# A two-direction RWKV recurrence: the triangular solve done beside its squarings, fewer and wider matmuls, steps without a loop

## The chip, the core and the metric

The program runs on one core of one Trainium2 chip. The metric is the time of one execution in device microseconds (us). Everything is float32. A float32 matmul stands in the program as one instruction and in the trace as two records (two MATMUL and two LDWEIGHTS); a transpose has one record of each.

## What is computed

The reference is two blocks in a row: a two-layer hybrid attention block, then a two-layer block with neighbourhood attention, an RWKV-7 mixer and two mixtures of experts. The change is inside the RWKV mixer of the second layer. It runs this step over 256 context tokens and then 512 latent tokens, in both directions, for 16 heads of 64, and uses outputs y of the latent tokens alone:

```python
def _rwkv_step(S, inp):
    r, w, kk, kka, kt, v = inp
    sk = jnp.einsum('bhij,bhj->bhi', S, kk)
    S = S * w[:, :, None, :] - sk[..., None] * kka[:, :, None, :] + v[..., None] * kt[:, :, None, :]
    return S, jnp.einsum('bhij,bhj->bhi', S, r)
...
        S_f, y_f = _rwkv_scan(S0[0], (r, w[0], kk, kk * a[0], kt[0], v), False)
        S_b, y_b = _rwkv_scan(S0[1], (r, w[1], kk, kk * a[1], kt[1], v), True)
        return (S_f, S_b), (y_f + y_b, r, kt, v, g)
...
    ctx_state, ctx_feats = stream(hc, None)
    _, lat_feats = stream(hl, ctx_state)
```

Here w is a decay per channel, kk the normalised key, a a learned rate, and `kka` is `kk * a`.

## The kernel before

`rwkv_layer` calls `rwkv_scan`, in which four engines work on chunks of 64 tokens (CH = 64): 4 of context, then 8 of latents, for each of two directions z, so 24 pairs of chunk and direction. The 16 heads are 8 pairs (PAIRS); two heads lie on partitions 0 to 63 and 64 to 127, and a product of all heads is 16 matmuls of 64x64 blocks (`heads`, line 2301, and `pair`, line 2290; line 2297 is the matmul itself). The work of one pair of chunk and direction has three parts.

- **front**: decays and rates of the chunk. `decay_rank` (L2339) and `rate_rank` (L2347) are low-rank products, `cumulate` (L2358) sums log-decays along the chunk, DVE adds biases (L2581, L2586), ACT takes sigmoids and exponentials with a table load ahead of each kind (L2500, L2511), and DVE and POOL scale keys and queries (L2594 to L2615, L2239 to L2248, L2260).
- **chain**: within a chunk the recurrence is a triangular system (I - N)X = X0, with N of 64x64 for each head. `gram` makes N and its transpose M from the keys, DVE masks them (L2647). Five `level` steps square them: each is 32 matmuls, 16 for the powers of N and 16 for those of M, and ACT (L2522) and DVE (L2651) copy the result from PSUM. POOL adds the identity to each power (`factor`, L2234), which gives the factors I + M^(2^n). `rows` turns keys by 32 matmuls with an identity, `raised_n` and `raised_r` are further grams.
- **tail**: `start` makes X0 from the carried state and the values; six `apply` steps multiply the factors into X one after another, each of 16 matmuls, an ACT copy (L2517) and the next; then `results` gives y and `state` the new state, which DVE adds (L2644) and POOL decays (L2253).

The order is written out by hand. A **slot** (the function `both`) holds the chain of one direction, the tail of the other and the front of the other's next chunk; each engine has its own list of the same steps. There are two slots per chunk, one for each direction. A hardware loop (`eng.Fori`, in `in_turn`, around L2185) runs two slots a turn, once over the context and once over the latents, with slots before and after each loop that fill and empty the pipeline. In a loop a semaphore wait is against a register value, and on PE each wait also adds to a semaphore `begun`; POOL copies the chunk's columns to fixed places first (L2220, L2222, L2227), since the loop's addresses change:

```python
            both(None, 0, 0, None, 0)
            both(0, 0, 1, None, 0)
            with eng.Fori(0, steps - 1) as it:
                both(1, it, 0, it, it + 1)
                both(0, it + 1, 1, it, it + 1)
            both(1, steps - 1, 0, steps - 1, None)
            both(None, 0, 1, steps - 1, None)
```

After the scan `rwkv_readout` normalises y and adds `bonus` times the values, and then output projection and experts follow. Stages are divided by a barrier of all engines, so the scan overlaps with no other stage.

## Time and profile before

| | |
|---|---|
| median of 3 runs | 4123.04 us (4122.61 to 4123.76) |
| the profiled execution, its own time | 4099.76 us |
| span of its trace | 4098.0 us |
| of it, the scan stage (2562.4 to 3376.2 us) | 813.8 us |
| mean granted TensorE clock | 0.91 |
| PE busy, DVE, ACT, POOL | 82%, 36%, 20%, 11% |

A stretch is named by its start and end in us from the span's start. A record's time is from its start to its modelled end, and matmuls overlap, so the time a group takes is read from its start to the start of what follows. The number in brackets at a row's end is the idle time of the engine before it and what ended it; "issue" is idle time for which the profile shows no awaited event. The granted clock is 1.00 at 2.4 GHz and 0.50 at 1.2 GHz.

### The profile page before, as it was taken

How to read it: one execution, taken by the hardware profiler on the slowest of the kernel's cores; microseconds unless marked ns; L12 is line 12 of the kernel's file. 1: busy time of each engine (PE TensorE's matmuls, PEld its weight loads, DVE VectorE, ACT ScalarE, POOL GpSimd, SP SyncE). 2: the span in 40 equal slices, each digit the busy share in tenths (PEclk: the TensorE clock that was granted, in tenths of full speed). 3: DMA queues.
4: the chain of work that ended last, by engine and by line, in shares of the span. 5: the costliest groups of instructions: out<-in, count | busy, mean ns of one | idle time of the engine just before them, and what ended most of it. 6: DMA issues, size and time to landing. Idle time of an engine off the chain costs nothing. (4 is left out here: it accounts for less than half of the span.)

```text
span 4098.0 us, 85586 instructions
## 1 busy us (share of the span) xinstructions
PE 3343.7 (82%) x37286; PEld 1973.3 (48%) x37286; DVE 1463.6 (36%) x3061; ACT 811.7 (20%) x1666; POOL 462.1 (11%) x448
## 2 busy tenths in 40 slices
PE   6998999896999986999995898776777765678877
PEld 5846476463445643343342444666666662322222
DVE  3656256552025623212213412443444434311111
ACT  2015111241015610000001001443333320100000
POOL 0000000000001100000000000443433320000000
PEclk9998899988999987999997998897989877799999
DMA  5652247302111124999996110000000002299998
GB/s 163 164 186 74 50 118 190 117 22 83 57 48 33 60 82 176 365 346 336 363 345 228 49 48 21 4 4 3 4 4 4 4 13 100 100 399 404 404 402 347
DMA packets 148963, 606.63 MB, mean 148 GB/s; under 512 B 19200, under 2 KB 21824, under 8 KB 131584
## 3 DMA queue, kind: packets, MB, share of 16 engines
q1 hardware_dynamic: 142272, 579.57, 39.0%
q0 software_dynamic: 6336, 21.63, 2.3%
q8 instruction: 308, 5.05, 0.5%
q14 instruction: 47, 0.39, 0.0%
HBM read 576.39 MB, written 31.07 MB: 148 GB/s over the span
## 5 line engine op out<-in xcount | busy, mean ns | idle before, releaser
L1704 PE MATMUL psum<-ring,big 128*64 128x512 f32 (+1 forms) x6144 | 904.8, 500 | 110.2 <-DMA ring<-moe_w 93.6
L1704 PEld LDWEIGHTS psum<-ring,big 128*64 128x64 f32 (+1 forms) x6144 | 301.4, 125 | 674.4 <-issue 472.6
L2297 PE MATMUL psum<-ring 64*64 64x64 f32 x11520 | 250.4, 232 | 100.8 <-issue 75.5
L371 PE MATMUL psum<-h_uT,ring 128*128 128x264 f32 x1280 | 290.5, 387 | 0.0
L2297 PEld LDWEIGHTS psum<-ring 64*64 64x64 f32 x11520 | 218.6, 143 | 129.2 <-issue 117.9
L371 PEld LDWEIGHTS psum<-h_uT,ring 128*128 128x128 f32 x1280 | 242.0, 190 | 46.5 <-issue 5.8
L500 DVE SCALAR_TENSOR_TENSOR h_O<-h_O,cond_silu 128x512 f32<-128x512 f32 x336 | 227.1, 743 | 102.2 <-DMA h_O<-ada_w 102.2
L1215 PE MATMUL psum<-ring,big 128*128 128x512 f32 x576 | 251.1, 596 | 2.0 <-PEq L55 2.0
L1985 PE MATMUL psum<-big,ring 128*128 128x512 f32 (+1 forms) x464 | 171.4, 532 | 31.7 <-DVE big L1956 24.0
L1850 DVE TENSOR_TENSOR big<-big,psum 128x512 f32<-128x512 f32 (+1 forms) x48 | 27.3, 596 | 463.7 <-PE psum L1704 463.7
L2234 POOL TENSOR_TENSOR ring<-ring,eye_sb 128x512 f32<-128x512 f32 x120 | 154.0, 1283 | 222.8 <-PE psum L2297 221.5
L1215 PEld LDWEIGHTS psum<-ring,big 128*128 128x128 f32 x576 | 109.0, 191 | 134.8 <-issue 134.8
L391 PE MATMUL psum<-ring,h_uT 128*128 128x512 f32 x384 | 168.3, 595 | 0.0
L2517 ACT ACTIVATE ring<-psum 128x512 f32<-128x512 f32 x168 | 100.4, 598 | 336.3 <-PE psum L2297 333.1
L1858 DVE SCALAR_TENSOR_TENSOR big<-psum,big,gates 64x512 f32<-64x512 f32 (+1 forms) x128 | 78.8, 615 | 242.8 <-PE psum L1704 241.4
L1001 PE MATMUL psum<-ring,big 128*128 128x512 f32 x320 | 141.3, 605 | 11.0 <-DMA ring<-rw_w_o 9.4
L1985 PEld LDWEIGHTS psum<-big,ring 128*128 128x128 f32 x464 | 90.0, 195 | 112.9 <-issue 108.8
L1784 ACT ACTIVATE big<-psum 128x512 f32<-128x512 f32 (+1 forms) x48 | 23.5, 524 | 566.8 <-PE psum L1704 566.7
L2651 DVE COPY ring<-psum 128x512 f32<-128x512 f32 x96 | 66.4, 691 | 173.7 <-PE psum L2297 173.7
L391 PEld LDWEIGHTS psum<-ring,h_uT 128*128 128x128 f32 x384 | 72.0, 190 | 90.2 <-issue 90.1
L119 PE MATMUL psum<-ident_sb,big 128*128 128x128 f32 x176 | 29.0, 343 | 97.0 <-DVE big L197 97.0
L1001 PEld LDWEIGHTS psum<-ring,big 128*128 128x128 f32 x320 | 61.9, 194 | 89.1 <-issue 79.6
(344 smaller groups left out, 4544.7 us busy)
## 6 DMA issues: line engine op xcount, KB each, us to landing
ring<-moe_w SPq DMA_DIRECT2D x192, 2048.0 KB, 10.8
h_O<-ada_w SPq DMA_DIRECT2D x192, 256.0 KB, 3.0
ring<-w_in SPq DMA_DIRECT2D x16, 2048.0 KB, 14.8
ring<-na_w_qkv SPq DMA_DIRECT2D x6, 2048.0 KB, 8.0
ring<-w_out SPq DMA_DIRECT2D x4, 2048.0 KB, 8.8
bias_rows<-na_table SPq DMA_DIRECT2D x16, 480.0 KB, 15.7
ring<-bias_rows SPq DMA_DIRECT2D x16, 360.0 KB, 2.9
rows<-big SPq DMA_DIRECT2D x10, 512.0 KB, 5.1
```

The lines of the kernel that those rows point to most:

```text
L371: last = nc.tensor.matmul(bank(k, pair_bank(q) + h, NH), w[:, a, f * P:(f + 1) * P], uT[:, a, halves[h]], start=a == 0, stop=a == KD - 1)
L391: last = nc.tensor.matmul(bank(k, b), uT[:, a, t * P:(t + 1) * P], w[:, a, :], **st)
L500: nc.vector.scalar_tensor_tensor(into, ada(u), by, into, ALU.mult, ALU.add).then_inc(s.acc, 1)
L1001: last = nc.tensor.matmul(bank(k, j % BANKS)[0:rows, :], srcT[:, a, t * P:t * P + rows], w[:, a, :], start=a == 0, stop=a == KD - 1)
L1215: last = nc.tensor.matmul(bank(k, j % FIRST_BANKS), hT[:, a, t * P:(t + 1) * P], w[:, a, :], start=a == 0, stop=a == KD - 1)
L1704: last = nc.tensor.matmul(bank(k, b, r.width)[q * r.n:(q + 1) * r.n, :], rowsT[:, half * HALF_K + n, r.first:r.first + r.n], w[:, n, q * r ...
L1858: last = nc.vector.scalar_tensor_tensor(y[r.first:r.first + r.n, x % 2, cols], bank(k, r.downs, r.width)[mine, :], gate[mine, x, 2 * r.at ...
L1985: last = nc.tensor.matmul(bank(k, j % BANKS, n), w[:, a, at:at + P], xs[m][:, a, first:first + n], **st)
L2234: ev["pool"][z].done(nc.gpsimd.tensor_tensor(pairs(factors[n], z), pairs(factors[n], z), eye3, ALU.add), f"factor{n}")
L2297: last = nc.tensor.matmul(bank(k, b, CH, at + p % QUAD * CH)[to:to + CH, :], pairs(lhs, z)[lo:lo + CH, p, :], rhs(lo, p), start=start and ...
L2517: ev["act"][z].done(nc.scalar.activation(flat2(T_n, z), side(W(z), 0), ACT.Copy), f"x{n}")
L2651: ev["dve"][z].done(nc.vector.tensor_copy(both_of(n, z, 1), bank(k, U(z) + 1).rearrange("p (e x) -> p e x", e=2)), f"level{n}")
```

## The change

- The solve is X <- X + M X beside the squaring of M and N: `level` n multiplies M by N and X, which lie side by side (one matmul of 128 columns per head block), and 16 matmuls of 64 columns give the next M. There are six levels; level 5 has X and M alone, level 6 X alone. The six `apply` steps and POOL's `factor` are gone. DVE adds the product to X in three operations (`step`), ACT copies M and N.
- `gram_m` and `raised` take alpha and rho side by side in 128 columns for latents; `gram_n` is a product of its own. `rows` is 8 transposes of 128x128 and six ACT copies in place of 32 matmuls and two copies. Bonus sums are 4 matmuls of 2 columns in place of 16 of one column.
- The loop, the register waits, `begun` and POOL's column copies are gone: all steps stand in the program one by one, with constant waits. The pipeline isn't emptied between context and latents. A slot now holds the solve of one direction (i), and of the other results and state (j), grams and start of the next chunk (n) and the front's first part of the one after (m).
- y and bonus are written by the first direction that comes to a chunk and added to by the second, so their fills are gone. `rwkv_readout` has four small ACT copies that put the bonus sums in order, for which POOL waits. Two more constant tables are loaded.

```diff
-            with eng.Fori(0, steps - 1) as it:
-                both(1, it, 0, it, it + 1)
-                both(0, it + 1, 1, it, it + 1)
...
+        def in_turn(slot):
+
+
+            here = lambda t: t if 0 <= t < ROUNDS else None
+            slot(1, None, None, 0, None, None, 0)
+            slot(0, None, 0, 1, None, None, 0)
+            slot(1, None, 0, 0, None, 0, 1)
+            for t in range(ROUNDS):
+                slot(0, t, here(t + 1), 1, here(t - 1), t, here(t + 1))
+                slot(1, t, here(t + 1), 0, t, here(t + 1), here(t + 2))
+            slot(0, None, None, 1, ROUNDS - 1, None, None)
...
-                def factor(z, it, n):
-
-                    after("pe", z, it, f"level{n + 1}")
-                    ev["pool"][z].done(nc.gpsimd.tensor_tensor(pairs(factors[n], z), pairs(factors[n], z), eye3, ALU.add), f"factor{n}")
-                    after("pool", z, it, f"factor{n}")
...
-                        last = nc.tensor.matmul(bank(k, b, CH, at + p % QUAD * CH)[to:to + CH, :], pairs(lhs, z)[lo:lo + CH, p, :],
-                                                rhs(lo, p), start=start and n == 0, stop=stop and n == len(terms) - 1)
+                        last = nc.tensor.matmul(bank(k, b, width, at + p % QUAD * width)[to:to + CH, :], lhs(lo, p), rhs(lo, p),
+                                                start=start and n == 0, stop=stop and n == len(terms) - 1)
...
-            pe.wait_ge(s.cleared, 3)
-            for lat, steps, first, chunk, ev, fr in phase_list():
-                def wait(sem, value):
-                    pe.wait_ge(sem, value)
-
-                    pe.sem_inc(s.begun, 1)
...
+            def gram_m(z, t):
+                made("dve", z, t, "rho" if lat(t) else "beta")
+                if lat(t):
+                    last = heads(W(z), 0, (beta(z), both(AR, z)), width=2 * CH)
+                else:
+                    last = heads(W(z), 0, (beta(z), alpha(z)))
+                ev["pe"][z].done(last, t, "gram_m")
...
+                for n, src in enumerate((T_beta, T_kappa)):
                     for i in range(QUAD):
...
+                        last = nc.tensor.transpose(bank(k, U(z) + n, P, i * P), own(src, z)[:, i * P:(i + 1) * P], k.ident[:, :])
+                ev["pe"][z].done(last, t, "rows")
...
+            def gram_n(z, t):
+                after("act", z, t, "rows")
+                ev["pe"][z].done(heads(U(z), 0, (alpha(z), beta(z))), t, "gram_n")
+
+            def level(z, t, n):
+
+
+                if n == 1:
+                    after("dve", z, t, "mask_n")
+                    after("dve", z, t, "x0")
+                else:
+                    after("dve", z, t, f"x{n - 1}")
+                    after("act", z, t, f"N{n - 1}" if n < LEVELS else f"M{n - 1}")
+                m = plain(T_m, z)
+                if n < LEVELS - 1:
+                    heads(U(z), 0, (m, with_x(z, n % 2 == 0)), width=2 * CH)
+                    last = heads(W(z), 0, (n_of(z), m))
+                elif n < LEVELS:
+                    heads(U(z), 0, (m, x_alone(z, n % 2 == 0)))
+                    last = heads(W(z), 0, (n_of(z), m))
+                else:
+                    last = heads(U(z), 0, (m, x_alone(z, n % 2 == 0)))
+                ev["pe"][z].done(last, t, f"level{n}")
...
-                def apply(z, it, n):
-                    after("act", z, it, f"x{n}")
-                    if n == 0:
-                        after("dve", z, it, "x0")
-                    if n < LAST:
-                        after("pool", z, it, f"factor{n}")
-                    else:
-                        after("dve", z, it, f"factor{n}")
-                    ev["pe"][z].done(heads(W(z), 0, z, (factors[n], of(T_n, z))), f"apply{n}")
...
-                def level(z, it, n):
-                    if n == 1:
-                        after("dve", z, it, "mask_m")
-                        made("pool", z, it, "end")
-                    else:
-                        after("act", z, it, f"level{n - 1}")
-                        after("dve", z, it, f"level{n - 1}")
-                    if n < LAST:
-                        heads(U(z), 0, z, (factors[n - 1], of(T_n, z)))
-                        last = heads(U(z), SIDE, z, (T_n, of(factors[n - 1], z)))
-                    else:
-                        last = heads(U(z), 0, z, (T_n, of(factors[n - 1], z)))
-                    ev["pe"][z].done(last, f"level{n}")
...
-                    if lat:
-                        made("dve", z, it, "rho")
-                    heads(W(z), 0, z, (T_beta, eye))
-                    ev["pe"][z].done(heads(W(z), SIDE, z, (T_kappa, eye)), "rows")
...
+            def slot(z, i, f, y, j, n, m):
+                if j is not None:
+                    results(y, j)
+                if n is not None and lat(n):
+                    bonus_sum(y, n)
+                if j is not None:
+                    state(y, j)
+                if i is not None:
+                    level(z, i, 1)
+                if m is not None:
+                    low_rank(y, m, j, n)
+                if i is not None:
+                    level(z, i, 2)
+                if n is not None:
+                    gram_m(y, n)
+                if i is not None:
+                    level(z, i, 3)
+                if m is not None:
+                    cumulate(y, m)
+                if i is not None:
+                    level(z, i, 4)
+                if n is not None:
+                    raised(y, n)
+                if i is not None:
+                    level(z, i, 5)
+                if n is not None:
+                    rows(y, n, j, m)
+                    start(y, n, j)
+                if i is not None:
+                    level(z, i, 6)
+                if n is not None:
+                    gram_n(y, n)
+
+            in_turn(slot)
...
+            def level(z, t, n):
+
+                after("pe", z, t, f"level{n}")
+                ev["act"][z].done(copy(groups(T_m, z), side(W(z), 0)), t, f"M{n}")
+                if n < LEVELS - 1:
+                    after("dve", z, t, f"xa{n}")
+                    copy(N(z)[:, 0, :, :], woven(U(z), 0)[:, 0, :, :])
+                    after("dve", z, t, f"x{n}")
+                    ev["act"][z].done(copy(N(z)[:, 1, :, :], woven(U(z), 0)[:, 1, :, :]), t, f"N{n}")
...
+            def rows(z, t):
+                after("pe", z, t, "rows")
+                for n, (to, sign) in enumerate(((T_brow, -1.0), (T_krow, 1.0))):
+                    got = bank(k, U(z) + n).rearrange("p (a h x) -> p h a x", h=2, x=CH)
+                    for rows, src, h in ((slice(0, P), slice(0, P), 0), (slice(CH, P), slice(0, CH), 1), (slice(0, CH), slice(CH, P), 1)):
+                        last = nc.scalar.activation(pairs(to, z)[rows, h * QUAD:(h + 1) * QUAD, :], got[src, h, :, :], ACT.Identity, scale=sign)
+                ev["act"][z].done(last, t, "rows")
+
+            def x_first(z, t):
+                after("pe", z, t, "start")
+                ev["act"][z].done(copy(X(z), side(W(z), 0)), t, "x0")
...
+            def step(z, t, n):
+                after("pe", z, t, f"level{n}")
+                got = woven(U(z), 1) if n < LEVELS - 1 else side(U(z), 0)
+                x = X(z)[:, 0, :, :]
+                ev["dve"][z].done(tt(x, x, got[:, 0, :, :], ALU.add), t, f"xa{n}")
+                if n == 1:
+                    after("dve", z, t, "x0")
+                else:
+                    after("dve", z, t, f"x{n - 1}")
+                old, new = x_of_side(z, n % 2 == 0), x_of_side(z, n % 2 == 1)
+                for h in range(2):
+                    here, there = slice(h * CH, (h + 1) * CH), slice((1 - h) * CH, (2 - h) * CH)
+                    last = tt(new[there], old[here], got[there, 1, :, :], ALU.add)
+                ev["dve"][z].done(last, t, f"x{n}")
+
```

PE, the middle of a latent slot in the loop of before: from level 4 to the end of the level 5 that closes the squarings; ring and gates hold the factors and keys, `head_ones_sb` is the bonus sum.

```order
L2297 MATMUL psum<-ring 64x64 x32
L2319 REGISTER_ALU x2
L2297 MATMUL psum<-ring 64x64 x16
L2319 REGISTER_ALU
L2297 MATMUL psum<-gates 64x64 x16
L2441 MATMUL psum<-head_ones_sb,ring 64x1 x16
L2319 REGISTER_ALU x2
L2297 MATMUL psum<-ring 64x64 x16
L2319 REGISTER_ALU
L2297 MATMUL psum<-ring 64x64 x16
```

PE, a latent slot in the program after: from level 1 to the end of `raised` and level 5's beginning; ring holds N and X, gates holds M, L2301 is the second low-rank product and L2312 is `cumulate`.

```order
L2256 MATMUL psum<-ring,gates 64x128 x16
L2256 MATMUL psum<-gates,ring 64x64 x16
L2297 MATMUL psum<-ring,X 64x512 x2
L2301 MATMUL psum<-X,ring 128x64 x8
L2256 MATMUL psum<-ring,gates 64x128 x16
L2256 MATMUL psum<-gates,ring 64x64 x16
L2256 MATMUL psum<-big,ring 64x128 x16
L2256 MATMUL psum<-ring,gates 64x128 x16
L2256 MATMUL psum<-gates,ring 64x64 x16
L2312 MATMUL psum<-running_sb,X 128x128 x8
L2256 MATMUL psum<-ring,gates 64x128 x16
L2256 MATMUL psum<-gates,ring 64x64 x16
```

Each level is now a row of 128 columns and a row of 64, with one step of the other direction between two levels, and no register instruction stands between.

DVE, the same loop of before: from `iclr` over a level's copy and `m` and `kt` to the next level's copy.

```order
L2586 TENSOR_TENSOR X<-psum,a_cols_sb 128x512
L2571 REGISTER_ALU
L2651 COPY ring<-psum 128x2x256
L2571 REGISTER_ALU
L2574 ISA
L2594 SCALAR_TENSOR_TENSOR ring<-X,ka_cols_sb 128x512
L2574 ISA
L2596 ISA
L2596 SCALAR_TENSOR_TENSOR ring<-ring,big 128x512
L2571 REGISTER_ALU
L2651 COPY ring<-psum 128x2x256
```

DVE, a latent slot after: step 1, then `dec`, `iclr`, `m`, `kt` and step 2.

```order
L2592 TENSOR_TENSOR ring<-ring,psum 128x4x64
L2600 TENSOR_TENSOR ring<-ring,psum 64x256 x2
L2522 TENSOR_TENSOR X<-psum,ring 128x512
L2527 TENSOR_TENSOR ring<-psum,a_cols_sb 128x512
L2535 SCALAR_TENSOR_TENSOR ring<-ring,ka_cols_sb 128x512
L2537 SCALAR_TENSOR_TENSOR ring<-ring,big 128x512
L2592 TENSOR_TENSOR ring<-ring,psum 128x4x64
L2600 TENSOR_TENSOR ring<-ring,psum 64x4x64 x2
L2586 TENSOR_TENSOR gates<-psum,before_less_sb 128x512
```

A level's single copy of 512 columns has become an addition of 256 columns on 128 partitions and two on 64 partitions, and four operations of the fronts stand between step 1 and step 2.

## Rows read from the trace of the kernel before

**Rows 1.** Stretches: length, busy (records) of PE, PEld, DVE, ACT, POOL; clock, DMA.

```profile
2562.40:2621.70 59.30, 42.50 (x1353) 36.41 (x1354) 28.62 (x39) 25.51 (x39) 26.25 (x26) 0.82 0.01 3
2621.70:2758.00 136.30, 100.81 (x4037) 89.23 (x4032) 63.09 (x86) 63.53 (x100) 53.96 (x56) 0.95 0.02 4
2758.00:2867.50 109.50, 76.21 (x2685) 67.42 (x2680) 41.54 (x60) 38.63 (x60) 41.25 (x39) 0.78 0.01 3
2867.50:3353.60 486.10, 352.50 (x13939) 319.81 (x13941) 206.56 (x317) 173.12 (x273) 182.68 (x178) 0.88 0.02 4
3353.60:3376.20 22.60, 12.64 (x383) 11.30 (x377) 2.98 (x6) 4.18 (x7) 2.06 (x2) 0.62 0.01 2
```

**Rows 2.** DMA queues, 2867.5 to 3353.6: packets, MB, share.

```profile
q8 instruction: 124, 2.03, 1.6%
```

**Rows 3.** PE in order of time, latent slot: start, length, group, count.

```profile
3057.76 1.20 PE L2297 MATMUL psum<-ring 64*64 64x64 f32 x46 [1.25 <-issue]
3059.05 1.16 PE L2358 MATMUL psum<-running_sb,ring 64*128 64x128 f32 x16
3060.14 1.15 PE L2297 MATMUL psum<-ring 64*64 64x64 f32 x60
3062.05 1.16 PE L2297 MATMUL psum<-ring 64*64 64x64 f32 x36 [0.76 <-issue]
3063.00 0.68 PE L2297 MATMUL psum<-big,gates 64*64 64x64 f32 x32
3063.47 0.67 PE L2297 MATMUL psum<-gates,big 64*64 64x64 f32 x32
3064.20 0.57 PE L2297 MATMUL psum<-ring 64*64 64x64 f32 x23
3066.21 1.53 PE L2297 MATMUL psum<-ring 64*64 64x64 f32 x73 [1.43 <-issue]
```

**Rows 4.** Who PE waited for, 2867.5 to 3353.6: us, times, longest.

```profile
PE psum L2297 <- issue: 68.2, 59, 2.1
```

**Rows 5.** PE at full clock in the first slots.

```profile
2581.61 2.00 PE L2347 MATMUL psum<-rw_tac,ring 64*128 64x64 f32 x16
2583.54 1.16 PE L2297 MATMUL psum<-ring 64*64 64x64 f32 x64
2584.52 0.65 PE L2297 MATMUL psum<-eye_sb,big 64*64 64x64 f32 x32
```

**Rows 6.** Transposes, `results`, `state`, `start`, first low-rank product.

```profile
33.77 6.66 PE L119 MATMUL psum<-ident_sb,h_O 128*128 128x128 f32 x39 [33.77 <-DVE h_O L197]
...
2567.41 1.97 PE L2339 MATMUL psum<-ring,rw_twc 64*64 64x512 f32 x4 [6.77 <-POOL rw_twc L2220]
...
3072.53 0.39 PE L2297 MATMUL psum<-X,gates 64*64 64x64 f32 x6 [0.80 <-ACT ring L2517]
...
3075.99 0.35 PE L2297 MATMUL psum<-X,big 64*64 64x64 f32 x7
...
3077.43 0.27 PE L2297 MATMUL psum<-X 64*64 64x64 f32 x2 [0.97 <-issue]
...
3078.47 0.34 PE L2297 MATMUL psum<-X 64*64 64x64 f32 x5
```

**Rows 7.** An `apply` alone, last slot: copy, then the next product.

```profile
3362.22 0.60 ACT L2517 ACTIVATE ring<-psum 128x512 f32<-128x512 f32 x1 [1.49 <-PE psum L2297]
...
3363.11 1.13 PE L2297 MATMUL psum<-ring 64*64 64x64 f32 x32 [0.95 <-ACT ring L2517]
```

**Rows 8.** Groups, by form: busy us, mean ns, idle before.

```profile
L2651 DVE COPY ring<-psum 128x512 f32<-128x512 f32 x96 | 66.4, 691 | 173.7 <-PE psum L2297 173.7
...
L1445 ACT ACTIVATE ring<-psum 128x256 f32<-128x256 f32 x32 | 10.3, 367 | 1.2 <-PE psum L1360 1.2
...
L2009 DVE COPY big<-psum 64x256 f32<-64x256 f32 x24 | 10.1, 422 | 73.3 <-PE psum L1982 73.1
L2640 DVE TENSOR_TENSOR ring<-ring,psum 128x256 f32<-128x256 f32 x24 | 10.1, 419 | 59.5 <-ACT ring L2517 59.5
```

786 lines of the change are left out of this document (347 added, 439 removed).

## Prediction

> **What bounds the kernel now.** I read the stretches first, then the queue of the DMA, then PE in order of time. The scan is a stage of its own, 2562.4 to 3376.2, 813.8 us [rows 1]; nothing else is touched but for trifles, so what it gains the kernel gains. Its slots can be counted by PE's records: a context slot has 402 matmuls, 804 records, so 4037 records in 136.3 us are 5 slots of 27.3 us; a latent slot has 498 matmuls, 996 records, so 13939 records in 486.1 us are 14 slots of 34.7 us [rows 1]. Between them, 109.5 us hold three slots, in which one loop ends and the other fills.
>
> PE has work for little more than 60% of a latent slot. Sixty-four records of 64x64 blocks, four blocks at a time, take 0.98 us from their start to that of the next group [rows 5], so 16 matmuls take 0.48 and 32 take 0.98. With the low-rank products at 1.97 and 1.93 [rows 5, 6], `results` and `state` at 3.46 with a short gap within, taken as 3.2, `start` at 2.82 less 0.97 idle = 1.85 [rows 6], and `cumulate` at 1.09 (3059.05 to 3060.14) [rows 3], the list of before sums to 3.2 + `gram` 0.98 + levels 4 x 0.98 + 0.48 + `rows` 0.98 + `raised_n` 0.98 + `raised_r` 0.9 + `apply` 6 x 0.48 + 3.9 + 1.09 + 1.85 = 21.2 us at full clock. The slot takes 34.7.
>
> The rest is in the gaps put down to "issue". They come in the middle of groups in which nothing is awaited, and evenly: 46 + 16 + 60 = 122 matmul records lie between the gap that ends at 3057.76 and that at 3062.05, and 36 + 32 + 32 + 23 = 123 between that and 3066.21 [rows 3]. With their weight loads that is some 245 instructions, and the instruction queue moved 124 packets in 486.1 us, 2.03 MB, 16.4 KB each [rows 2]. At 64 bytes an instruction (an estimate from 16.4 KB and the 256 that the gaps suggest) each is a page of 256. So PE gets a page each 3.92 us, uses it up in some 2.3 us where all is dense, and stands for the rest: 68.2 us in 59 gaps, 1.16 us each [rows 4]. A latent slot takes 124 / 14 = 8.9 pages, and 8.9 x 3.92 is 34.7: the whole slot. The supply of instructions bounds the loop, and the waits of the solve lie hidden in it.
>
> **Part 1: fewer instructions.** A latent slot after has 366 matmul instructions, 8 of them transposes: 358 x 4 + 8 x 2 = 1448 records, and the register instructions are gone (8.9 x 256 = 2270 less 1992 leaves 280 of them before). With some 30 waits that is 5.8 pages, 22.7 us by 3.92. A context slot has 314: 1270, 5.0 pages, 19.5 us. Pages alone would no longer bound either.
>
> **Part 2: PE's work.** Sixteen matmuls of 128 columns cost at least 0.48 (as many instructions as the narrow ones) and about 0.98 at most (the columns of 32 narrow ones) [rows 5]. I take 0.92, near the upper end, since the columns double and only weight loads are saved. Eight transposes of 128x128: 6.66 / 39 = 0.17 each [rows 6], 1.4 in all, 0.4 more than the 32 matmuls of before. Latent slot: 3.2 (`results`, `state`) + 0.3 (bonus, between 0.1 and 0.6) + levels 1 to 4 at 0.92 + 0.48 each, 5.6, + 0.98 + 0.48 + 3.9 + `gram_m` and `raised` 1.84 + 1.09 + 1.4 + 1.85 + `gram_n` 0.48 = 21.1. So PE's work stays what it was; context 21.1 - 2.1 (`results`) - 0.3 - 0.88 = 17.8.
>
> **Part 3: the waits that take the place of the gaps.** Level n + 1 needs X and N of level n: 0.06 us from PE's end to the copy, and 0.29 from the copy's end (3362.82) to the next product (3363.11) [rows 7]. Between them now stand three DVE additions of 256 columns, one on 128 and two on 64 partitions, at 0.42 each, and the last ACT copy of 256 columns, 0.37 [rows 8]: 0.06 + 1.26 + 0.37 + 0.29 = 1.98, and 0.16 more, by which a group of 16 matmuls ends after the next could start (0.65 against 0.49) [rows 5]: 2.14. What stands between on PE hides part of it. Level 1 to 2: the low-rank products, 3.9, hide all. Level 2 to 3: `gram_m` 0.92 hides all but 1.22, and DVE comes late by about 0.6, since `iclr`, `m` and `kt` stand ahead of step 2. Level 3 to 4: `cumulate`, 1.04 left. Level 4 to 5: `raised`, 1.22 left. Level 5 to 6: transposes and `start` hide all. At the end, ACT has six copies for `rows` and one for X0, DVE adds X0 and only then takes step 6, and `results` waits for that, some 1.5. Together 5.6: 26.7 us. In a context slot `gram_m` and `raised` hide 0.44 less each: 17.8 + 6.5 = 24.3.
>
> **Part 4: what is left of the page limit.** From `start` over level 6, `gram_n`, `results`, bonus and `state` to the end of level 1 there are 180 matmuls, 720 instructions, 2.8 pages, 11.0 us, against 1.85 + 0.96 + 1.5 + 3.5 + 1.4 = 9.2 us of work and wait: 1.8 more. In a context slot 128 matmuls, 2.0 pages, 7.8 against 6.8: 1.0. Elsewhere a page holds wide matmuls and waits and lasts about 4 us anyway. The granted clock was 0.88 in the latent stretch, 0.95 in the context [rows 1]; PE will stand less, and I add 0.3 and 0.2. So a latent slot is **28.8 us** and a context slot **25.5 us**.
>
> **Part 5: ends of the pipeline.** Before, the first state came 59.3 us after the stage's start [rows 1]. After, the fills of y and bonus go, but three filling slots stand first; with the first solve I put the first state there as well, so 35 us ahead of the first of 24 solving slots. At the end only results, state and y are left, 6 us. The turn between the loops is two ordinary slots and more in before, none of it lost in after. POOL loses `factor` and the column copies, off the path. The ACT copies in the readout are under 0.4 each and POOL, which waits, has nothing behind it that is late; two table loads and they cost 1 us at most.
>
> Sum: 35 + 8 x 25.5 + 16 x 28.8 + 6 = 706 us against 813.8, 108 less. The profiled execution took 4099.76 and would take 3992. The median of the runs is 4123.04, 0.6% above it, and the same difference from it gives **4015 us**.
>
> **Where the Trainium skill disagrees.** The Trainium skill ("Runtime: NRT & Kernel Launch", Instruction fetch mechanics) says that crossing into the next 16 KiB block is mostly hidden by the fetch ahead, and that a taken branch is what stalls it. The gaps in the loop show otherwise: a turn is two slots, 17.7 pages, with one jump, and a gap stands at nearly every page [rows 2, 3]. By that rule the gaps would leave with the loop.
>
> **Rivals.**
> - *The gaps belong to the loop.* Its jumps and register instructions make them, and straight code has none. Then part 4 falls away: slots of 27.0 and 24.5, 35 + 196 + 432 + 6 = 669, **3978 us**. For it: all gaps that I read lie in a loop. Against it: their even distance. Then each of 5.8 pages costs its 1.2 us beside the waits: 26.7 + 0.3 + 7.0 = 34.0, and 24.3 + 0.2 + 6.0 = 30.5: 35 + 244 + 544 + 6 = 829, **4138 us**. It decides from about 5.5 us of gaps in a mean slot: (813.8 - 41) / 24 = 32.2, against 26.1 without gaps. For it: in before, work and gaps do add up to most of the slot. Against it: a wait within a page gives the fetch time.
> - *DVE's narrow additions cost as much as wide ones*, 0.69 for 0.42 [rows 8], by their strides and by waits in DVE's order. A step is 0.8 longer, at four places: 32.0 and 28.7, 35 + 230 + 512 + 6 = 783, **4092 us**. Against it: both rows of 256 columns.
> - *All falls well.* Wide products at 0.48, no page limit, full clock: 24.9 and 22.5, 35 + 180 + 398 + 6 = 619, **3928 us**.
>
> **Chances.** Forecast 0.55 (3975 to 4060 of its own), gaps of the loop 0.12, DVE's price 0.12, gaps added 0.11, all well 0.10. The range reaches from part of the last case over the first three to 4100 and leaves out 4138: 3950 to 4100. About 0.2%, 8 us, is what a measurement tells from no change. Faster by more 0.86, within it 0.03 (between DVE's price and the added gaps), slower 0.11.
>
> **What the profile after would show.** Part 1: 5.8 and 5.0 packets of instructions a slot. Part 2: PE's records of 128 columns, 32 in about 0.92 us, and 8 transposes in 1.4. Part 3: PE waiting for DVE's `step` or ACT's N copy at levels 3, 4 and 5 and ahead of `results`, 1.1 to 1.9 us each. Part 4: gaps of "issue" between `start` and level 1, and few between levels. I am wrong if gaps of 1.2 us stand at every page still, if DVE is busy for most of a slot, or if the clock falls below 0.8.

## The result, and the profile after

The kernel after takes **3940.9 us** (median of four runs, 3931.4 to 3953.5) against 4123.4 (four runs, 4122.6 to 4124.0): a ratio of 0.9559, with a 95% interval of 0.9526 to 0.9593. The forecast was 4015 with a range from 3950; the time lies 9 us below the range. The direction and the engine that bounds were right, the gain is 182 us where 108 were forecast.

Its profiled execution took 3932.92 us, span 3931.1. The scan goes from 2561.8 to 3215.7: 653.9 us against 813.7, so 160 of the 167 us between the two profiled executions are there. The windows of both scans and of the stretches after, with the columns of [rows 1]; the first is of before, the others of after (the whole scan; five slots, nearly all of them context; thirteen latent slots, the first twelve of them full):

```profile
2562.40:3376.10 813.70, 584.66 (x22368) 524.16 (x22368) 342.78 (x504) 304.96 (x479) 306.19 (x299) 0.87 0.02 4
```

```profile
2561.80:3215.70 653.90, 503.71 (x16544) 450.01 (x16544) 411.16 (x816) 330.80 (x647) 116.57 (x105) 0.94 0.01 3
...
2628.30:2748.10 119.80, 88.94 (x3100) 79.77 (x3100) 75.68 (x152) 69.12 (x136) 14.80 (x16) 0.96 0.01 3
...
2798.50:3146.90 348.40, 277.38 (x9371) 250.29 (x9372) 232.85 (x466) 176.86 (x348) 74.97 (x66) 0.96 0.01 4
```

A slot is best counted from one decay of the state to the next, POOL's operation on `d_end` (once a slot). POOL in order of time, after: the first slot, the beginning and the end of twelve full latent slots, and the last two.

```profile
2628.30 1.04 POOL L2211 TENSOR_TENSOR X<-X,rw_d_end 128x512 f32<-128x512 f32 x1
...
2798.49 1.04 POOL L2211 TENSOR_TENSOR X<-X,rw_d_end 128x512 f32<-128x512 f32 x1
...
3122.81 1.04 POOL L2211 TENSOR_TENSOR X<-X,rw_d_end 128x512 f32<-128x512 f32 x1
...
3191.05 1.04 POOL L2211 TENSOR_TENSOR X<-X,rw_d_end 128x512 f32<-128x512 f32 x1 [24.98 <-DVE X L2583]
3214.63 1.04 POOL L2211 TENSOR_TENSOR X<-X,rw_d_end 128x512 f32<-128x512 f32 x1 [22.54 <-DVE X L2583]
```

(3122.81 - 2798.49) / 12 = **27.0 us** a full latent slot, where 28.8 was forecast. Those in which the granted clock stays at 1.00 take 26.0 to 26.2, those at 0.94 take 27.5. The seven slots ahead take 24.3 on average (25.5 forecast), the shortest of them 23.0, and the last four 23.0 on average (17.9 to 26.3), since less and less of a front is in them (28.8 forecast, as if they were full).

The queue of instructions, 2748.1 to 3144.4 (15 slots, 12 of them full), against 124 packets in 486.1 us [rows 2]; and whom PE waits for there, against 68.2 us of "issue" [rows 4]:

```profile
q8 instruction: 84, 1.38, 1.4%
```

```profile
PE psum L2256 <- ACT ring L2443: 52.9, 46, 2.0
PE psum L2256 <- DVE ring L2600: 20.8, 13, 1.6
PE psum L2256 <- ACT X L2480: 6.1, 15, 0.4
```

The gaps that nothing ended are gone. What stands in their place are the waits of the solve: for ACT's copy of N (L2443), for DVE's step 6 (L2600) ahead of `results`, and a new short one for ACT's copies of rows (L2480). PE in order of time in one latent slot shows them one by one, beside the prices of the new shapes [rows 5]:

```profile
2957.32 1.10 PE L2256 MATMUL psum<-ring,gates 64*64 64x128 f32 x32 [1.46 <-ACT ring L2443]
2958.24 0.64 PE L2256 MATMUL psum<-gates,ring 64*64 64x64 f32 x32
2958.81 1.16 PE L2312 MATMUL psum<-running_sb,X 64*128 64x128 f32 x16
2960.82 1.10 PE L2256 MATMUL psum<-ring,gates 64*64 64x128 f32 x32 [0.84 <-ACT ring L2443]
...
2964.31 0.69 PE L2256 MATMUL psum<-ring,gates 64*64 64x64 f32 x32 [1.05 <-ACT ring L2443]
...
2965.40 1.09 PE L2348 MATMUL psum<-ident_sb,ring 128*128 128x128 f32 x8
2966.42 0.36 PE L2256 MATMUL psum<-X,big 64*64 64x64 f32 x8
...
2968.92 0.69 PE L2256 MATMUL psum<-ring,big 64*64 64x64 f32 x32 [0.41 <-ACT X L2480]
2971.21 0.39 PE L2256 MATMUL psum<-X,big 64*64 64x64 f32 x6 [1.60 <-DVE ring L2600]
...
2973.22 1.05 PE L2320 MATMUL psum<-head_ones_sb,X 128*128 128x2 f32 x8
2974.20 0.34 PE L2256 MATMUL psum<-ring,X 64*64 64x64 f32 x8
...
2976.53 0.61 PE L2297 MATMUL psum<-ring,X 64*64 64x512 f32 x2
...
2977.49 2.00 PE L2301 MATMUL psum<-X,ring 64*128 64x64 f32 x16
2979.41 1.10 PE L2256 MATMUL psum<-ring,gates 64*64 64x128 f32 x32
```

The waits are 1.46 + 0.84 + 1.05 + 0.41 + 1.60 = 5.4 us of 26.0. The bonus sums (L2320) take 0.98 us (2973.22 to 2974.20) for matmuls of two columns. PE's weight loads show why: the other side of each is 128x128, and loading it fills that time.

```profile
2973.22 0.97 PEld L2320 LDWEIGHTS psum<-head_ones_sb,X 128*128 128x128 f32 x8
```

### The profile page after: what moved, and what is told of

Read it like the earlier page. It is cut to its first block and busy times, and to the rows that moved or that the text cites. A ratio compares the mean times of both kernels' runs of the same rounds, so it can differ in the third digit from the quotient of the medians.

```text
span 3931.1 us, 72090 instructions
## 1 busy us (share of the span) xinstructions
PE 3256.2 (83%) x31462; PEld 1895.5 (48%) x31462; DVE 1528.8 (39%) x3373; ACT 838.0 (21%) x1838; POOL 276.4 (7%) x254
## 5 line engine op out<-in xcount | busy, mean ns | idle before, releaser
L1704 PE MATMUL psum<-ring,big 128*64 128x512 f32 (+1 forms) x6144 | 902.6, 500 | 115.2 <-DMA ring<-moe_w 99.0
L2256 PE MATMUL psum<-ring,gates 64*64 64x128 f32 (+1 forms) x5120 | 177.2, 265 | 96.5 <-ACT ring L2443 94.1
L2256 PEld LDWEIGHTS psum<-ring,gates 64*64 64x64 f32 x5120 | 140.0, 141 | 111.0 <-DVE ring L2600 108.4
L1215 PEld LDWEIGHTS psum<-ring,big 128*128 128x128 f32 x576 | 109.0, 191 | 134.8 <-issue 134.8
L1784 ACT ACTIVATE big<-psum 128x512 f32<-128x512 f32 (+1 forms) x48 | 23.5, 524 | 565.5 <-PE psum L1704 565.5
L2600 DVE TENSOR_TENSOR ring<-ring,psum 64x256 f32<-64x256 f32 x288 | 120.9, 420 | 6.4
L2443 ACT ACTIVATE gates<-psum 128x512 f32<-128x512 f32 x120 | 71.6, 596 | 236.0 <-PE psum L2256 236.0
L1790 ACT ACTIVATE big<-psum 128x512 f32<-128x512 f32 (+1 forms) x48 | 25.2, 526 | 399.8 <-PE psum L1727 399.8
L2256 PE MATMUL psum<-big,ring 64*64 64x64 f32 (+1 forms) x2816 | 110.3, 249 | 0.0
```

The source lines that it names most:

```text
L1215: last = nc.tensor.matmul(bank(k, j % FIRST_BANKS), hT[:, a, t * P:(t + 1) * P], w[:, a, :], start=a == 0, stop=a == KD - 1)
L1704: last = nc.tensor.matmul(bank(k, b, r.width)[q * r.n:(q + 1) * r.n, :], rowsT[:, half * HALF_K + n, r.first:r.first + r.n], w[:, n, q * r ...
L2256: last = nc.tensor.matmul(bank(k, b, width, at + p % QUAD * width)[to:to + CH, :], lhs(lo, p), rhs(lo, p), start=start and n == 0, stop=st ...
L2443: copy = lambda out, got: nc.scalar.activation(out, got, ACT.Copy)
L2600: last = tt(new[there], old[here], got[there, 1, :, :], ALU.add)
```

## Experiments

Two theories stand against each other for the kernel before: **P**, the forecast's, that PE is held by the supply of instruction pages wherever its code is dense, and **L**, that the gaps belong to the loop. For the kernel after, **S** says that the chain of the solve sets the slot. Times are medians, ratios to the kernel before, run on the same chip beside them. The groups of runs stood on different chips: the kernel before took 4123.4 us beside after, 4132.9 beside E1 to E4, 4124.1 beside E5 to E8 and 4132.4 beside E9 to E11. So across groups the ratios count and not the medians; 0.001 of a ratio is 4.1 us.

| | us | ratio (95%) | scan, us | clock in it |
|---|---|---|---|---|
| before, first profile / second (E9) | 4123.4 | 1 | 813.7 / 844.6 | 0.87 / 0.83 |
| after | 3940.9 | 0.9559 (0.9526 to 0.9593) | 653.9 | 0.94 |
| E1 before, written out | 4080.6 | 0.9865 (0.9844 to 0.9886) | 796.5 | 0.87 |
| E2 before, four slots a turn | 4074.2 | 0.9856 (0.9832 to 0.9881) | 792.4 | 0.88 |
| E3 after, narrow | 3982.0 | 0.9628 (0.9603 to 0.9652) | 694.3 | 0.93 |
| E4 after, M first | 3864.9 | 0.9344 (0.9324 to 0.9363) | 585.5 | 0.95 |
| E5 as E4, step 6 first | 3849.8 | 0.9338 (0.9313 to 0.9362) | 554.0 | 0.97 |
| E6 after, DVE early | 3923.4 | 0.952 (0.9491 to 0.9549) | 636.7 | 0.92 |
| E7 after, less DVE | 3882.4 | 0.942 (0.9392 to 0.9449) | 595.0 | 0.97 |
| E8 after, dense | 4082.2 (one run) | | 794.4 | 0.95 |
| E10 after, `m` and `kt` first | 3941.2 | 0.9542 (0.9519 to 0.9566) | 660.6 | 0.92 |
| E11 as E5 and E10 | 3844.2 | 0.9313 (0.9294 to 0.9332) | 558.4 | 0.96 |

### E1: the loop alone

```diff
-            with eng.Fori(0, steps - 1) as it:
+            for it in range(steps - 1):
                 both(1, it, 0, it, it + 1)
                 both(0, it + 1, 1, it, it + 1)
```

> The kernel before, with the scan's hardware loops written out: the same matmuls in the same order, constants in the place of register values in the waits; the increments of `begun` and the copies of columns stay. A latent slot is then 1992 matmul instructions and some 70 waits and increments, 2060, or 8.05 pages of 256 (8.9 before); a context slot 1670, 6.5 pages. Theory P (the prediction's: a page of instructions each 3.92 us, wherever the code stands): slots of 31.5 and 25.6 us against 34.7 and 27.3, the scan about 750 us against 813.8, the kernel 0.984 of before; gaps of issue still stand at nearly every page, some 1.1 us each. Theory L (the gaps belong to the loop): the gaps that no event ends leave PE almost wholly, 68.2 us of them in 14 slots, 4.9 us a slot; what they hid of the waits comes back in part. Slots of 29 to 30 us, the scan 700 to 730, the kernel 0.975 to 0.982; issue gaps under 10 us in the 14 slots, and pages that follow each other sooner than 3.9 us where the code is dense.

The kernel gains 1.35%, 52 us by the medians of one chip. The gaps stay. Whom PE waits for in 14 latent slots (2869.1 to 3336.1) of E1:

```profile
PE psum L2297 <- issue: 82.2, 71, 2.1
PE psum L2339 <- POOL rw_twc L2220: 20.9, 13, 2.1
PE psum L2297 <- ACT ring L2517: 11.1, 14, 0.8
PE psum L2441 <- issue: 8.7, 5, 1.9
PE psum L2358 <- issue: 2.8, 2, 1.4
```

Together 93.7 us of issue in 14 slots, in code without one jump, against 68.2 + 17.8 = 86.0 in before (the row of the sums of bonus, below, belongs to [rows 4]). Theory L falls: the gaps don't belong to the loop. 110 packets in these slots are 7.9 pages a slot, as counted (8.05). But P's times missed too: the scan is 796.5 us where P said 750, a latent slot 33.4 where it said 31.5. The pages came 4.25 us apart on average (467.0 / 110) and not 3.92, and beside the gaps stand 33 us of waits for POOL, ACT and DVE. So the gaps belong to the supply of pages, but the supply doesn't set the whole slot.

P's account of the gain doesn't hold either. It came from 0.85 page a slot of register instructions. Of before, the same stretch as [rows 4], the other rows:

```profile
PE psum L2441 <- issue: 17.8, 13, 1.6
PE psum L2297 <- POOL rw_tac L2222: 12.2, 3, 4.3
...
PE psum L2297 <- POOL rw_twc L2220: 10.7, 3, 3.7
```

and PE around one turn of the loop:

```profile
2966.66 0.33 PE L2297 MATMUL psum<-X,ring 64*64 64x64 f32 x6
2971.29 0.51 PE L2297 MATMUL psum<-X,big 64*64 64x64 f32 x8 [4.29 <-POOL rw_tac L2222]
```

Each turn of the loop stands for some 4 us, six times in these slots, 22.9 us. The profile names POOL's copy, but the group that starts is `start`, which doesn't wait for that copy. Over the whole scan the profile puts eight such stands, 30.3 us, down to POOL's copies, one for each of the eight jumps back. In E1 these stands are gone, and part of them comes back elsewhere in the 14 slots: PE waits 20.9 us for POOL's copy ahead of the low-rank product (9.1 before), and issue gaps are 7.7 us more. By the Trainium skill ("Runtime: NRT & Kernel Launch", Instruction fetch mechanics) a taken branch whose target lies outside the two pages at hand forces a fetch of it before execution goes on; a stand of 4 us at each turn agrees with it, and is about what one page takes in E8 (3.74 us). The same section's rule that crossing a 16 KiB block is mostly hidden does not agree with E1's 93.7 us in straight code.

### E2: half the jumps

```diff
-            with eng.Fori(0, steps - 1) as it:
-                both(1, it, 0, it, it + 1)
-                both(0, it + 1, 1, it, it + 1)
+            both(1, 0, 0, 0, 1)
+            both(0, 1, 1, 0, 1)
+            with eng.Fori(0, (steps - 2) // 2) as turn:
+                for u in (1, 2):
+                    it = turn * 2 + u
+                    both(1, it, 0, it, it + 1)
+                    both(0, it + 1, 1, it, it + 1)
```

> The kernel before, with four slots in a turn of the loop and not two, so half the jumps back (the first two slots of each loop are written out ahead of it). P: nothing changes but for trifles, a page still takes 3.92 us: 0.998 to 1.002 of before. If it is the jump that stops the supply: half of the gaps go, 2.4 us a slot, 40 to 50 us of the kernel, 0.988 to 0.990. If anything in a loop is supplied late, however long the turn: no change in the loop's slots, but the slots written out run without gaps, some 3 us less each, four of them: 0.996 to 0.998.

All three expectations missed: 59 us less by the medians, as much as without a loop. The two loops jump back twice in place of eight times (2 + 6), so six jumps less were worth as much as eight within the measurement, which doesn't tell them apart. The gaps of issue in the latent slots (76.2 + 1.8 us in 14 slots) are near those of before, so a jump has its own price, beside the pages and not instead of them: two stands of this kind are left in the scan for the two jumps, 8.1 us, where before had eight and 30.3. The instruction queue moved 182 packets in the scan, E1's 179 and before 194: 12 less for six jumps, so a jump also costs some two pages fetched for nothing. The stands account for 22 us of the 59. The scans of the profiled pair differ by 21 us against the first profile of before and by 52 against the second (E9), and the second difference is mostly PE's busy time at a higher granted clock (574.6 us at 0.88 against 612.4 at 0.83); why the clock is higher no run shows.

### E3: more instructions for the same columns

```diff
-                        last = nc.tensor.matmul(bank(k, b, width, at + p % QUAD * width)[to:to + CH, :], lhs(lo, p), rhs(lo, p),
-                                                start=start and n == 0, stop=stop and n == len(terms) - 1)
+                        for e in range(width // CH):
...
+                            last = nc.tensor.matmul(bank(k, b, CH, at + p % QUAD * width + e * CH)[to:to + CH, :], lhs(lo, p), r,
+                                                    start=start and n == 0, stop=stop and n == len(terms) - 1)
```

> The kernel after, with each matmul of 128 columns split into two of 64 on the same weights: 96 more matmuls in a latent slot, 384 instructions, 1.5 pages more (7.1), 64 more in a context slot, 1.0 page (5.8 to 6). P: a page each 3.92 us gives 27.8 us for a latent slot against 26.4, and the dense stretch from start to the end of level 1 gets 0.25 page longer; with gaps of issue back: 20 to 35 us more than after. L, with the solve's waits as the bound: only PE's work grows, 32 blocks of 64 columns in 0.98 us against 0.92, six times, 0.4 us or less a slot, some of it behind waits: 0 to 10 us more than after, no issue gaps.

41 us slower than after by the medians, 28 by the ratios (0.9628 against 0.9559: 0.0069 x 4123; the kernel before was 10 us slower beside E3), the scan 40 us longer. Gaps of issue are back. Some twelve latent slots of E3 (2798 to 3146):

```profile
PE psum L2260 <- ACT ring L2447: 21.7, 25, 1.5
PE psum L2260 <- issue: 20.8, 27, 2.0
PE psum L2260 <- DVE ring L2604: 18.8, 12, 1.6
PE psum L2316 <- issue: 3.3, 3, 1.3
PE psum L2305 <- issue: 1.1, 1, 1.1
```

That is the upper end of P's 20 to 35 and beyond by the medians, within it by the ratios. 25.2 us of gaps in 348, and 87 packets, a page each 4.0 us. Part of the gaps lies where the waits for ACT were (21.7 us here; 45.0 in the same stretch of after). P holds, and says what the wide products are worth: not PE's work (0.92 against 0.98 for a group) but a quarter of the instructions.

### E4: the chain shortened, M first

```diff
+                if n < LEVELS:
+                    ev["pe"][z].done(heads(W(z), 0, (n_of(z), m)), t, f"m{n}")
+                after("dve", z, t, f"x{n - 1}")
                 if n < LEVELS - 1:
-                    heads(U(z), 0, (m, with_x(z, n % 2 == 0)), width=2 * CH)
-                    last = heads(W(z), 0, (n_of(z), m))
+                    last = heads(U(z), 0, (m, with_x(z, n % 2 == 0)), width=2 * CH)
...
-                after("pe", z, t, f"level{n}")
-                ev["act"][z].done(copy(groups(T_m, z), side(W(z), 0)), t, f"M{n}")
+                after("pe", z, t, f"m{n}")
+                ev["act"][z].done(copy(groups((T_m, T_m2)[n % 2], z), side(W(z), 0)), t, f"M{n}")
```

> The kernel after, with each level's product for M ahead of that for N and X, a second buffer for M (so that ACT copies M beside the second product), and ACT's copy of N in the order that keeps clear of DVE (the far half first). The values are the same. Theory S (the chain of the solve, from a product's end over ACT and DVE to the next, sets the slot): the next product can begin when N is there, 0.37 + 0.37 + 0.06 + 0.29 = 1.1 us after the level's end, and X, ready 1.6 after it, is awaited behind 0.48 of work; before it was 2.1. The waits ahead of levels 3, 4 and 5 (1.46, 0.84, 1.05) fall by up to 1.0, 0.84 and 1.0: a latent slot of 23.6 to 24.4 us against 26.4, a context slot 21.5 to 22.5 against 24.0, 45 to 65 us less than after. P: 5.6 pages by 3.92 are 22.0, but the dense stretches grow, and gaps of issue come back: a latent slot not under 25, 20 to 30 us less than after.

The second buffer for M lies over the gate that the projection after the scan multiplies with, so that what follows the scan works on other values, at the same cost. 76 us less than after by the medians, 89 by the ratios (0.9344 against 0.9559), 68 in the scan: the way S says, and more than its 45 to 65. The edit holds three things (M first, its second buffer, the order of ACT's copies), which no run takes apart. Full latent slots take 23.7 to 24.3 us for the most part, as S says, and context slots 20.7, less than its 21.5 to 22.5. PE in order of time around `raised` and the end of a slot:

```profile
2975.85 0.69 PE L2256 MATMUL psum<-gates,ring 64*64 64x64 f32 x32 [0.44 <-ACT ring L2440]
...
2982.97 0.59 PE L2256 MATMUL psum<-X,big 64*64 64x64 f32 x6 [1.60 <-DVE ring L2599]
...
2995.54 0.69 PE L2256 MATMUL psum<-gates,ring 64*64 64x64 f32 x32 [0.48 <-ACT ring L2440]
```

Level 3 waits 0.48, level 4 nothing and level 5 0.44, in place of 1.46, 0.84 and 1.05: 2.4 us less a slot. Hardly a gap of issue comes back (0.3 us in 375), so after had room down to this. `results` still waits 1.60.

### E5: step 6 ahead of X0

```diff
+                if i is not None:
+                    step(z, i, 6)
                 if n is not None:
                     after("act", y, n, "x0")
                     x = joint(NX, y, 1)[:, QUAD:, :]
                     ev["dve"][y].done(tt(x, x, bank(k, W(y), SIDE, SIDE).rearrange("p (a x) -> p a x", x=CH), ALU.add), n, "x0")
-                if i is not None:
-                    step(z, i, 6)
```

> The same as the kernel with the product for M first, but the second buffer for M lies in columns of Y and V that are free at that time (in the former run it lay over a gate that a later stage needs), and DVE takes step 6 of the one direction ahead of the addition to X0 of the other. Theory S: `results`, which waited 1.60 us for step 6 in each slot, finds it ready 0.42 us of addition and some 0.7 us of waiting for ACT's copy sooner: 1.0 us less in each of 23 slots, 20 to 26 us less than the former run's 3865. Theory P, with the shortest distance of two pages seen so far, 3.35 us, as the true price: 5.6 pages are 18.8 us, still under the slot, but between `start` and the end of level 1 2.8 pages are 9.4 us, and with a wait of 0.5 in the place of 1.6 the work there is 9.0: gaps of 0.4 us come back in some slots, and 10 to 16 us are left of the gain.

3849.8 us. The wait ahead of `results` falls from 1.60 to 0.50, as S says:

```profile
2910.20 0.69 PE L2262 MATMUL psum<-ring,big 64*64 64x64 f32 x32 [0.23 <-ACT X L2483]
2911.39 0.39 PE L2262 MATMUL psum<-X,big 64*64 64x64 f32 x6 [0.50 <-DVE ring L2605]
```

The scan is 31.5 us shorter than E4's, of which 1.1 us in 23 slots are 25. The kernel is 15 us faster by medians from two chips, but the ratios, 0.9338 against 0.9344, differ by 2 us and their intervals overlap, and the profiled execution (3834.0) was the fastest of the five. So the profile shows the wait shrink, and the timed runs don't show that the kernel gains by it. The expected 20 to 26 us aren't borne out. A full latent slot takes 22.6 to 23.9 us.

### E6: DVE doesn't wait for the product of M

```diff
-                    heads(U(z), 0, (m, with_x(z, n % 2 == 0)), width=2 * CH)
+                    ev["pe"][z].done(heads(U(z), 0, (m, with_x(z, n % 2 == 0)), width=2 * CH), t, f"u{n}")
...
-                after("pe", z, t, f"level{n}")
+                after("pe", z, t, f"u{n}" if n < LEVELS else f"level{n}")
```

> The kernel after, with one event more a level: DVE takes up its step when the product for N and X is done and doesn't wait for the product for M behind it. ACT still waits for both. S: DVE is 0.48 us sooner where it isn't busy, and the chain is then ACT's: copy of M 0.60, two of N 0.37 each, 1.34 after the level's end, against 1.63; 0.28 less at levels 4 and 5, nothing at level 3, where DVE comes late from `m` and `kt`, 0.3 less ahead of `results` no (level 6 has one product): 0.5 to 0.6 us a slot, 10 to 15 us less than after. If PE isn't bound by this chain: no change.

17.5 us less than after by the medians, 16 by the ratios, somewhat above the 10 to 15 of S; the intervals of the two ratios overlap a little, so the gain is likely and not certain. Level 4 waits 0.37 and level 5 0.58, so 0.47 less each where 0.28 was reckoned, and level 3 as before:

```profile
2898.36 1.10 PE L2256 MATMUL psum<-ring,gates 64*64 64x128 f32 x32 [1.45 <-ACT ring L2443]
2901.39 1.10 PE L2256 MATMUL psum<-ring,gates 64*64 64x128 f32 x32 [0.37 <-ACT ring L2443]
2904.41 0.69 PE L2256 MATMUL psum<-ring,gates 64*64 64x64 f32 x32 [0.58 <-ACT ring L2443]
2911.31 0.39 PE L2256 MATMUL psum<-X,big 64*64 64x64 f32 x6 [1.59 <-DVE ring L2600]
```

I had added ACT's durations, but its operations overlap: in the profile of after a copy of N starts 0.49 us after a copy of M that lasts 0.60.

### E7: one addition less a step

```diff
-                for h in range(2):
+                for h in range(1):
                     here, there = slice(h * CH, (h + 1) * CH), slice((1 - h) * CH, (2 - h) * CH)
```

> The kernel after, with one of the two additions on 64 partitions left out of each step (half of X on one side isn't updated, so the output isn't the recurrence's). Each step is 0.42 us shorter on DVE. S: 0.42 less ahead of level 3 (DVE is the late one) and of `results`, 0.28 less ahead of levels 4 and 5, where ACT's last copy of N, which waits for the step, is then held by ACT's own two copies: 1.2 to 1.4 us a slot, 28 to 34 us less than after. If the slot is bound by pages or by PE's work: 0 to 5 us.

58 us less than after, the scan 59: more than S's 28 to 34. The waits fall by 0.43 (1.03 at level 3), 0.44, 0.43 and 0.60, 1.9 us a slot, since ACT's own two copies weren't in the way and DVE comes sooner everywhere. Full latent slots take 24.3 to 25.2, and context slots 21.3. That is some 44 us in 23 slots. The clock is 0.97 against 0.94, and PE is busy 17 us less for the same records (486.4 against 503.7), which gives the rest. So DVE's steps are on the chain at all four places.

### E8: dense code, to read the price of a page

```diff
-                ev["pe"][z].done(heads(U(z), 0, (alpha(z), beta(z))), t, "gram_n")
+                for _ in range(9):
+                    last = heads(U(z), 0, (alpha(z), beta(z)))
+                ev["pe"][z].done(last, t, "gram_n")
```

> The kernel after, with the product `gram_n` issued nine times and not once, each time into the same place, so the values are the same: 128 matmuls, 512 instructions, 2.0 pages and 8 x 0.48 = 3.84 us of PE's work more in a slot, without a wait among them. They hide the 1.60 us that `results` waited. Without any limit by pages a latent slot is then 26.4 + 3.84 - 1.6 = 28.6 us and a context slot 26.2. P with 3.92 us a page: from `start` to the end of level 1 stand 4.8 pages, 18.8 us, against 12.3 of work: a latent slot of 33 to 35 us, gaps of some 1.8 us at each page there. P with 3.35 us a page, the shortest distance of two pages that any run shows, and the next page fetched ahead while PE still waits elsewhere: 16.1 us in that stretch less what was fetched ahead, a latent slot of 30.5 to 32.5, and pages in the dense stretch that follow each other in 3.3 to 3.4 us.

Full latent slots take 31.3 to 33.9, with two of 36: between the two prices. In the dense stretch the gaps of before are back:

```profile
2957.47 2.94 PE L2256 MATMUL psum<-ring,big 64*64 64x64 f32 x183 [0.42 <-ACT X L2482]
2962.06 1.78 PE L2256 MATMUL psum<-ring,big 64*64 64x64 f32 x105 [1.65 <-issue]
...
2965.80 0.27 PE L2256 MATMUL psum<-big,ring 64*64 64x64 f32 x1 [1.54 <-issue]
```

From the end of one gap to that of the next are 3.74 us. In the dense stretches of this slot and the next the packets on the instruction queue come 3.4 to 3.8 us apart. So the price of 3.92 was somewhat too high and 3.35 too low. 183 matmul records of one product run through before the first gap, nearly half again a page's worth of some 128, so at least one end of a page passed without a stand: it follows that a page fetched ahead lay ready. In the next slot the first gap comes after 94 records and is shorter (1.11 us), so what is in store depends on where the page ends.

### E9: the kernel before once more

> The kernel before, unchanged, profiled once more. Its timed executions in these comparisons lie between 4103 and 4141 us, and the profiled one from which the prediction was made took 4099.76, 23 us under their median. If the scan is what varies, its 813.7 us are longer here, with more or longer gaps of issue; if it is the stages that stream weights, the scan stays within 3 us and the rest, 3284 us, is longer. An execution like the first shows neither.

4133.7 us, with a scan 30.9 us longer than in the first profile, for the same records:

```profile
2568.80:3413.40 844.60, 612.43 (x22368) 550.76 (x22368) 342.27 (x504) 305.66 (x479) 304.55 (x299) 0.83 0.02 4
```

PE is busy 27.8 us longer (584.66 in the first), the clock 0.83 against 0.87. Its waits by "issue" are not more (123.4 us against 120.8). So between these two the scan differs by PE's busy time at a lower granted clock and not by gaps, and the execution from which the forecast was made was one of the quick ones. What sets the clock lower, they don't show.

### E10 and E11: DVE's `m` and `kt` at the slot's start

```diff
+                if f is not None:
+                    keys(z, f)
                 if j is not None and lat(j):
                     results(y, j)
...
                 if m is not None:
                     low_rank(y, m)
-                if f is not None:
-                    keys(z, f)
```

> The kernel after, with DVE's two operations `m` and `kt` at the start of the slot, where DVE waits for `results`, and not between step 1 and step 2. By the prediction DVE comes 0.6 us late to step 2 for them. S: step 2 begins at the level's end, and the wait ahead of level 3 falls from 1.46 to 1.0: 0.4 to 0.5 us a slot, 9 to 12 us less than after, 3940.9. If ACT and not DVE holds that wait, or POOL's next steps come too early for it: no change, within 3 us.

The wait moves as S says, 1.46 to 1.06 at level 3:

```profile
2911.55 1.10 PE L2256 MATMUL psum<-ring,gates 64*64 64x128 f32 x32 [1.06 <-ACT ring L2443]
```

The kernel doesn't: 3941.2, and its scan is 6.7 us longer. PE waits 36.6 us for ACT's copy between 2798 and 3146, 8.4 less than after, but is busy 6.4 us more in the same 348 us at a clock of 0.95 against 0.96. Over the whole scan:

```profile
2565.50:3226.10 660.60, 517.75 (x16544) 461.38 (x16544) 428.12 (x816) 329.34 (x647) 122.13 (x105) 0.92 0.01 3
```

PE has 14 us more of busy time for the same records (503.71 in after) at 0.92 against 0.94. So the clock took the gain back in this execution. Whether it does so in every one, one profile can't say.

> The product for M first, step 6 ahead of the addition to X0, and `m` and `kt` at the slot's start, all three in one kernel. In the kernel with the first two DVE comes late to step 2 by 0.5 us and more, and PE waits 0.5 at levels 3 and 5 for ACT's copy, which waits for DVE. S: 0.3 to 0.5 us less in a slot, 7 to 12 us less than 3849.8. P: a slot of 22.6 us holds 5.6 pages, and by 3.8 us a page, the distance in the dense stretches of the kernel with `gram_n` nine times, these take 21.3: near the bound, so half of that or less, 0 to 5 us, with more gaps of issue.

3844.2 us against E5's 3849.8, and intervals of the ratios that overlap: the two can't be told apart, so this run doesn't decide between S's 7 to 12 us and P's 0 to 5. Gaps of issue are 2.5 us in 375 (2765 to 3140), in E5 2.0, so P's "more gaps" isn't seen. By the ratios E5 beats the kernel after by 91 us and E11 by 101.

## Why the prediction was wrong

It missed by 74 us. Set beside the profiled execution they come apart so: 52 us in the scan (706 forecast, 653.9 measured), 7 outside it (3284.3 against 3277.2 us; other profiles, of kernels alike there, lie between 3275.0 and 3287.3), and 16 from the step from the profiled difference (167) to that of the medians (182).

- **What bounds before.** Right in its core: the supply of pages holds PE in dense code. E1 keeps the gaps without a loop, E3 and E8 bring them back into the kernel after by instructions alone. Wrong in one piece: the 8.9 pages a slot were not 280 register instructions but in part pages thrown away at the loop's jumps, which have a price of their own. And the sum that was to show that pages bound the whole slot, 8.9 x 3.92 = 34.7, shows nothing: 3.92 is 486.1 / 124 and 8.9 is 124 / 14, so their product is the length of the slot whatever bounds it. E1, with 4.25 us a page in the same code without jumps, shows that waits stand beside the gaps. Leaving the loop is worth 1.35% (E1), 56 us; the rest of the 182, some 126 us, comes from fewer instructions and the shorter solve.
- **Part 1, pages.** Right: the 12 full latent slots have 68 packets, 5.7 each (5.8 forecast), and the context has 24 in five, 4.8 (5.0).
- **Part 2, PE's work.** 21.1 forecast, 26.0 - 5.4 = 20.6 measured. The wide group takes 0.92, as taken. Transposes take 1.02 (1.4 forecast), `start` 1.40 (1.85), the first low-rank product 0.96 (1.97, which was read at 2567.41, where the granted clock of before is 0.50), the bonus sums 0.98 (0.3): four matmuls of two columns load weights of 128x128, which takes 0.97 us. Groups priced 1.9 us too dear (the low-rank product 1.0, `start` 0.45, the transposes 0.4) stand against bonus sums 0.7 too cheap, so that the total came out so near is in part luck.
- **Part 3, the waits.** Right: 5.6 forecast, 5.4 measured, at the places named: 1.46, 0.84, 1.05 and 1.60 against 1.8, 1.04, 1.22 and 1.5; and 0.41 at `gram_n`, which wasn't named. E4 and E7 show that they are the bound, and E6 points the same way.
- **Part 4, what is left of the page limit.** This step failed. 1.8 us in a latent slot and 1.0 in a context slot were added for the stretch from `start` to the end of level 1, 2.8 pages by 3.92 against 9.2 of work. The stretch takes 10.1 us (2966.42 to 2976.53), all work and named waits, without a gap, so the term measured nothing. It makes 36 of the 52 us: 1.8 in each of 16 latent slots and 1.0 in the seven ahead. Work and wait there were priced 0.9 too low, and the supply too harshly. Around the stretch packets moved on the instruction queue at 2966.4, 2972.4 and 2976.2: the first came as the stretch began, the next only 6.0 us later, behind the two waits in it, and the third 3.8 us after that, no closer than in E8. So the stretch asks for two pages after its beginning and not for 2.8, and never faster than they come. The price alone isn't the error: 2.8 pages at E8's 3.74 are 10.5 us, still more than 10.1. E8 with two pages more does feel the price. The forecast multiplied a rate by a length and left out what is in store.
- **The clock.** 0.3 us a slot forecast, 27.0 - 26.0 = 1.0 measured. In the comparison it helped all the same: 0.94 in the scan against 0.87 and 0.83. E9 shows what such a step can be worth, 28 us of PE's busy time for 0.04.
- **Part 5, the ends.** Also wrong. The last four slots take 91.9 us (3122.81 to 3214.63), where four full ones, 115.2, were forecast: 23 us. Less and less of a front and at last no next chunk is in them. The first state comes 66.5 us after the start, 6 later than forecast; after the last there is 1 us and not 6.
- **The sum of the scan.** 12 full latent slots 1.8 each, 21; the last four 23, of which 7 are part 4's; seven slots ahead 1.2 each, 8; the ends -1: 52 us with rounding.
- **The base.** The forecast took the difference of one execution to the median. E9 shows that the profiled one had 31 us less of scan than another, which took 4133.7. If the executions near the median have the longer scan too, more is saved from them than from the profiled one; the timed executions have no trace, so this stays open.
- **The rivals.** "Gaps belong to the loop" came nearest by its slots (27.0 and 24.5), for a wrong reason: straight code has gaps too (E1), and they went because the code asks for a page each 4.7 us (396.3 / 84) and the supply gives one in 3.7 to 3.8. "All falls well", 3928, came nearest in total, but its wide products at 0.48 weren't so. Gaps that add to the waits had no gaps to add here; in dense code they do in part (E1). DVE's narrow additions at 0.69 fall: 0.41 to 0.42 each.

## What to carry to other kernels

When PE has gaps that nothing ended in the middle of dense groups, count instructions, not columns: a product of twice the columns costs the same work and half the pages, and a page for each four to five microseconds of work and wait came free here. Once pages don't bound, look at what stands between two dependent products: issuing the product that needs the least first, with a buffer of its own and the copies in a fitting order, was worth 76 to 89 us here (E4). The order of two steps on the engine behind it took 1.1 us off a wait in each slot (E5), but the timed runs show no gain from it. A rate got by dividing a length by a count is no price: read it where nothing else can hold the engine, as in E8. And price the slots in which a pipeline fills and empties by what is in them, and take the profile of the kernel before twice if its time isn't near the median.
